# VectorE's split of the second and third weight tile moved behind the next block step's masks, in a fused two-block transformer kernel

## The reference, cut to what matters

```
z = einsum('bhqd,bhkd->bhqk', qb, kb)
log_keep = where(before, log_sigmoid(-z), 0)
log_stick = cumsum(log_keep, axis=3, reverse=True) - log_keep
w = where(before, exp(log_sigmoid(z) + log_stick), 0)
out = einsum('bhqk,bhkd->bhqd', w, vb)
```

## Time and profile before

| | |
|---|---|
| median of 3 runs | 1793.81 us (1793.61 to 1793.97) |
| the profiled execution, its own time | 1793.58 us |
| its span, first to last instruction | 1791.9 us |
| TensorE busy (matmul) | 1761.8 us, 98% of the span |
| VectorE busy | 1153.6 us, 64% |
| ScalarE busy | 845.8 us, 47% |
| mean granted TensorE clock | 0.998 of full speed |
| stick stage, block steps 0 to 15 and their tail | about 1424.8 to 1543.7 us of the span |

### The profile page before, as it was taken

How to read it: one execution, slowest core, us unless ns; L and a number is a source line. 1 busy time by engine, 2 the same in 40 slices (tenths; PEclk the granted TensorE clock), 3 DMA queues, 4 the chain that set the end, 5 groups by cost and what they waited for, 6 DMA issues and landing times.

```text
span 1791.9 us, 23591 instructions
## 1 busy us (share of the span) xinstructions
PE 1761.8 (98%) x8174; PEld 1388.8 (78%) x8174; DVE 1153.6 (64%) x1826; ACT 845.8 (47%) x1311; POOL 34.4 (2%) x61
## 2 busy tenths in 40 slices
PE   9999999899999999999999999999999999999998
PEld 6787777678888888888887788888887765677886
DVE  7888888567777743377777677776433556665444
ACT  6555555444444432267777444444322465643222
POOL 1000000000000000000000000000000000100000
PEclk9999999999999999999999999999999999999999
DMA  5522122022222142143331222222321312223221
GB/s 198 167 70 70 59 70 59 36 96 95 93 94 93 59 155 88 62 132 106 103 114 65 94 94 94 94 94 84 124 97 52 106 36 71 92 78 99 100 93 60
DMA packets 45816, 163.26 MB, mean 91 GB/s; under 512 B 5841, under 2 KB 8164, under 8 KB 45760
## 3 DMA queue, kind: packets, MB, share of 16 engines
q1 hardware_dynamic: 40864, 148.00, 24.7%
q0 software_dynamic: 4464, 14.47, 2.9%
q10 hardware_dynamic: 432, 0.07, 0.0%
HBM read 155.89 MB, written 6.63 MB: 91 GB/s over the span
## 4 chain that ended last, share of the span: by engine, by line
PE 91%; DVE 4%; ACT 3%; issue 1%; DMA 0%; SPq 0%; DVEq 0%; ACTq 0%
PE acc L587 23%; PE acc L588 23%; PE acc L589 23%; PE acc L613 8%; ACT wsplit L1170 1%; PE pbc L750 1%; PE pbc L954 1%; PE pbc L733 1%; PE pa L587 1%; PE pa L588 1%; PE pa L589 1%; DVE wsplit L1712 1%; PE pbc L1029 1%; PE pa L712 1%; PE pd L967 1%
## 5 line engine op out<-in xcount | busy, mean ns | idle before, releaser
L587 PE MATMUL acc<-xhi,wsplit 128*128 128x512 f32 x1200 | 487.5, 406 | 1.4 <-DVE at_vs L2155 1.3
L1170 ACT ACTIVATE wsplit<-wraw 128x1024 fp32r<-128x1024 f32 (+1 forms) x252 | 276.3, 1097 | 442.6 <-PE acc L589 408.6
L589 PE MATMUL acc<-xhi,wsplit 128*128 128x512 f32 x1200 | 475.5, 396 | 0.0
L588 PE MATMUL acc<-xlo,wsplit 128*128 128x512 f32 x1200 | 475.5, 396 | 0.0
L1712 DVE TENSOR_TENSOR wsplit<-wraw,wsplit 128x1024 fp32r<-128x1024 f32 (+1 forms) x249 | 317.0, 1274 | 158.9 <-ACT wsplit L1170 158.0
L587 PEld LDWEIGHTS acc<-xhi,wsplit 128*128 128x128 f32 x1200 | 225.9, 188 | 68.7 <-issue 14.0
L589 PEld LDWEIGHTS acc<-xhi,wsplit 128*128 128x128 f32 x1200 | 225.9, 188 | 54.7
L588 PEld LDWEIGHTS acc<-xlo,wsplit 128*128 128x128 f32 x1200 | 226.4, 189 | 51.4 <-issue 1.4
L613 PE MATMUL acc<-xhi,wsplit 128*128 128x512 f32 x464 | 157.8, 412 | 0.0
L588 PE MATMUL acc<-hid_lo,wsplit 128*128 128x512 f32 x352 | 139.6, 396 | 0.0
L589 PE MATMUL acc<-hid_hi,wsplit 128*128 128x512 f32 x352 | 139.6, 396 | 0.0
(11 more groups left out here) (390 smaller groups left out, 2542.2 us busy)
## 6 DMA issues: line engine op xcount, KB each, us to landing
wraw<-w SPq DMA_DIRECT2D x220, 512.0 KB, 3.3
wraw<-w SPq DMA_DIRECT2D x32, 704.0 KB, 4.1
bias_dram<-ext_dram POOLq DMA_DIRECT2D x1, 4096.0 KB, 20.8
bias<-bias_dram POOLq DMA_DIRECT2D x16, 256.0 KB, 3.0
at_ks<-at_ks SPq DMA_DIRECT2D x16, 256.0 KB, 2.9
crow<-row_dram POOLq DMA_DIRECT2D x8, 256.0 KB, 3.8
brow<-row_dram POOLq DMA_DIRECT2D x8, 256.0 KB, 4.3
h<-xT SPq DMA_DIRECT2D x3, 512.0 KB, 8.2
```

The source lines that it names most:

```text
L587: mm(out, whi[:, k, :], a[:, x_at + k, :], start=(k == first), stop=False)
L588: mm(out, whi[:, k, :], b[:, x_at + k, :], start=False, stop=False)
L589: m = mm(out, wlo[:, k, :], a[:, x_at + k, :], start=False, stop=(k == last))
L1170: A(split(s, i, j, 0), raw(s, j), ACT.Copy).then_inc(w_hi_ready, 1)
```

## The change

VectorE's subtractions for tile 1 and tile 2 of a pair are put one block step later each. Tile 0 stays where it was (v = 2). Tile 1 moves from the end of step v = 3 to the end of the next step, v = 0, and tile 2 from v = 0 to v = 1. The same holds for the three tiles of the `sgu` stage that are prepared during the last pairs. Nothing is added or removed, and no other engine's program differs.

```diff
                     if ahead and v in (1, 2):
                         take(i + 1, v - 1)
-                    if ahead and v in (2, 3):
-                        low_ahead(s, i + 1, v - 2, i + 1 == SBP - 1)
-                    if 0 < i < SBP and v == 0:
-                        low_ahead(s, i, 2, i == SBP - 1)
+                    if ahead and v == 2:
+                        low_ahead(s, i + 1, 0, i + 1 == SBP - 1)
+                    if 0 < i < SBP and v < 2:
+                        low_ahead(s, i, v + 1, i == SBP - 1)
                     if step == blocks - 1:
```

## The result

| | before | with the change |
|---|---|---|
| median of 11 runs each | 1793.81 us (1793.42 to 1795.17) | 1789.37 us (1788.80 to 1789.52) |
| the profiled execution, its own time | 1793.58 us | 1789.06 us |
| its span | 1791.9 us | 1787.4 us |
| TensorE busy | 1761.8 us | 1759.3 us |
| stick stage, first logits to the next stage's first transposes (line 1058) | 118.85 us | 114.29 us |

A forecast was written before the change was run, and what follows sets the result against it. TensorE, holding 91% of the chain that ended last, was taken as the bound. Terms 0.75 + 1.35 + 2.06 + 0.22 + 0.2 = 4.58 us off 1793.58 gave 1789.00, plus 0.23 for the median: 1789.2 us, range 1788.5 to 1790.6.

The forecast's parts named there:

- Three waits go: TensorE's waits for VectorE's carry before the suffix sums of steps 4, 8 and 12 were to vanish.
- the terms 0.75, 1.35 and 2.06: Microseconds to be regained on TensorE at steps 4, 8 and 12, counted from start to start.
- The 0.11: Extra us from suffix sums to next product in each waiting step, expected back; 0.33 less gain if not.
- The rival by the idle column: Only the drawn idle of steps 4, 8 and 12 comes back: 3.34 us, so 1790.5 us; chance 8%.
- The two small terms, 0.22 and 0.2: Step 13: suffix sums 0.22 us sooner and product by values about 0.2 sooner, as the correction precedes tile 2's subtraction.
- The fourth wait stays: Step 16's wait, 1.17 us of drawn idle, remains, since its softplus waits for ScalarE and not for a subtraction.
- Tile 1 in time: Step 4: tile 1's subtraction ends about 1452.4, TensorE wants it at 1456.5; 4.1 us to spare, no cost.
- My rival in the prediction: Tile 1 comes too late, each us late costing one in each of three pairs: 1797.4 us or more; chance 3%.
- points of decision: With tile 1 over 4.1 us late, 1.5 us more uses up the gain; 2.7 more makes it slower by over 0.2%.
- the later loads: SyncE's raw tile loads go out some 2.5 to 5 us later, claimed to cost nothing.

The follow-up runs named there:

- the run on the last pair: The change made for the last pair alone (steps 11 to 13), against the kernel before: 1791.03 us, ratio 0.9986.
- The run with tile 1 only: Tile 1's subtraction moved behind the mask of v = 0, tile 2's left in v = 0 right behind it: 1788.95 us, ratio 0.9971 to the kernel before.
- The runs on it: Three kernels against the changed one: ScalarE's step 14 rounding earlier, 1788.41 us; step 16's third dense product before the suffix sums, 1788.68 us; both, 1787.87 us.
- tile 1 later still: The changed kernel with tile 1's subtraction moved on to step v = 1, behind the softplus and before the mask: 1790.48 us, ratio 0.9981 to the kernel before.

## Why the prediction was right, point by point

The time, the sign and the mechanism held, and most terms of the sum could be read off afterwards.

- **Three waits go.** Each last dense start to the next product is 1.55 (step 4), 1.54 (step 8) and 2.04 us (step 12), by the rows above; the sum used 1.54, 1.54 and 2.04. So the terms 0.75, 1.35 and 2.06 stand, to 0.01.
- **Start to start, not the idle column.** The 0.11 that I took back from each wait came back: unhindered sums at 512 wide take 1.32 and 1.31 to the next product, where no row before had shown it. The Trainium skill's rule of weight loads pulled ahead (TensorE: Matmul & The Clock Gate, Step-by-step: what each phase is for) fits the changed kernel, whose load for step 12 starts at 1509.32, 0.22 ahead of its matmul at 1509.54; in the kernel before both started at 1513.51. The rival by the idle column, 3.34 us, is out by the run on the last pair.
- **Step 13.** The two small terms, 0.22 and 0.2, came to 0.43 together (suffix sums 0.23 behind the dense product, the next 0.54 behind these). But I credited them to tile 2's move. The run with tile 1 only shows the same length without it: with tile 1 out of the way ScalarE rounds tile 2 earlier, and there is nothing left for its move to mend. Either move removes the 0.43, so the term was right in size and not tied to the cause I gave.
- **The fourth wait stays**, at 1.18, ScalarE's share. The runs on it show that it could be mended, by other edits.
- **Tile 1 in time.** The subtraction ends at 1452.39 and the tile is wanted at 1456.61: 4.2 us to spare, 4.1 reckoned. The run that uses it up costs what was expected of that run, 1.32 us. My rival in the prediction had counted such a delay in each of three pairs; it shows in two, and step 12, whose tile by that run's expectation is wanted two steps later, has none, so its points of decision (1.5 and 2.7 us) were too early.
- **One step was wrong without cost.** I said of the later loads that they "are for the pair after, a turn of about 30 us. Nothing." For the first tile of the next stage this is false: ScalarE waits 3.0 us for it in step 9. It costs nothing (the stage is 114.27 us in the run with tile 1 only, where this wait is absent) only because 2.2 us are left behind it at the exponential. That margin was in no step of the prediction; that it was enough was luck. I had read the order of the loads inside the stage, not what SyncE waits for at its border.

The sum of the terms was 4.58; the stage is 4.56 shorter, and the medians differ by 4.44.

## What to carry to other kernels

An instruction that waits in an in-order queue holds up everything behind it, so price the wait by what stands behind it and not by its own length: here the same 4.6 us came from moving the waiting instruction behind the urgent ones or from doing what it waits for earlier. Count a stall of TensorE from one start to the next, against an unhindered case of the same kind, since the drawn idle of the three waits (3.34 us) was a fifth short of what they cost (4.16, worked out from starts; together with step 13's 0.43 it is 4.59, and the stage gained 4.56). And when a release is moved later, follow the transfer queue across the stage's border: its wait there can be on the last release of the stage, and the margin can be one step.

## What the runs showed that I had not expected

- The subtraction of tile 2, moved alone, shortens the stage by 0.44 us, and moved on top of tile 1 by nothing (114.29 against 114.27 us): the value of an edit here depends on which other one is made.
- A dense product that waited 0.6 us for VectorE's half of its weights is booked as `issue`, 0.44 us, in the profile of the kernel with tile 1 later still.
- A first load that was issued 4.25 us later, counted from the logits of its step, put ScalarE in a 3.0 us wait, and one step later in 6.5 us; the first cost nothing and the second 1.40 us of the stage.
